# FFN input blocks of a two-layer decoder trunk: one 512-column matmul for the rounded weights instead of two of 256

## What is computed

```
for l in (0, 1):
    h = h + 0.5 * swiglu(rms_norm(h, ffn1_norm), ffn1_w_in, ffn1_w_out)
    u = rms_norm(h, mix_norm)
    ...  four mixers on projections of u, gated, summed over branches
    h = h + mixed @ w_out
    h = h + 0.5 * swiglu(rms_norm(h, ffn2_norm), ffn2_w_in, ffn2_w_out)

swiglu(u): a, b = split(u @ w_in);  (silu(a) * b) @ w_out        # width 2816 inside
```

## Time and profile before

| | us |
|---|---|
| median of 3 runs | 1290.23 (1284.02 to 1292.07) |
| the profiled execution, as timed | 1289.22 |
| its span in the trace | 1287.3 |
| PE busy | 1245.8 (97%) |
| DVE busy | 895.5 (70%) |
| ACT busy | 640.0 (50%) |
| PE's waits on w_lo_t, the longest kind | 15.0, of them 14.1 at the start |

### The profile page before, as it was taken

How to read it: one execution, slowest core, us unless ns; L and a number is a source line. 1 busy time by engine, 2 the same in 40 slices (tenths; PEclk the granted TensorE clock), 3 DMA queues, 4 the chain that set the end, 5 groups by cost and what they waited for, 6 DMA issues and landing times.

```text
span 1287.3 us, 25597 instructions
## 1 busy us (share of the span) xinstructions
PE 1245.8 (97%) x10328; PEld 1222.4 (95%) x10328; DVE 895.5 (70%) x1172; ACT 640.0 (50%) x904; POOL 327.4 (25%) x462
## 2 busy tenths in 40 slices
PE   5999999999999999999999999999999999999998
PEld 5999999888999999999999999998889999999998
DVE  4766857877877676555676687687887786656554
ACT  5654545663544454444456445557625444534432
POOL 0388800364003300000005895005630041000000
PEclk9999999998999999999999999999999999999999
DMA  7555554542344365555545545544333454555541
GB/s 299 199 185 174 180 179 165 175 149 99 131 158 166 135 236 198 191 195 168 191 135 201 188 165 200 189 164 152 135 130 131 154 186 160 201 184 175 186 173 66
DMA packets 31029, 220.46 MB, mean 171 GB/s; under 512 B 3568, under 2 KB 3568, under 8 KB 4592
## 3 DMA queue, kind: packets, MB, share of 16 engines
q1 hardware_dynamic: 30960, 219.49, 49.0%
HBM read 218.42 MB, written 1.05 MB: 170 GB/s over the span
## 4 chain that ended last, share of the span: by engine, by line
PE 75%; DVE 12%; POOL 7%; ACT 3%; issue 2%; DMA 0%; DVEq 0%; SPq 0%; ACTq 0%
PE banks L456 24%; PE banks L457 24%; PE banks L458 24%; DVE w_lo_t L1072 5%; PE banks L469 3%; ACT w_hi_t L812 1%; POOL st L1631 1%; DVE s5x L1274 1%; POOL s5x L1629 1%; POOL s5x L1628 1%; POOL st L1634 1%; POOL st L1536 1%; POOL st L1632 1%; DVE u_lo_t L1084 1%; DVE hT L1223 1%
## 5 line engine op out<-in xcount | busy, mean ns | idle before, releaser
L1072 DVE TENSOR_TENSOR w_lo_t<-raw,w_hi_t 128x1024 fp32r<-128x1024 f32 x408 | 518.0, 1310 | 107.8 <-ACT w_hi_t L812 107.4
L812 ACT ACTIVATE w_hi_t<-raw 128x1024 fp32r<-128x1024 f32 x408 | 407.2, 1046 | 126.7 <-PE banks L458 126.0
L456 PE MATMUL banks<-u_hi_t,w_hi_t 128*128 128x256 f32 x1520 | 436.0, 287 | 18.2 <-DVE w_lo_t L1072 14.1
L457 PE MATMUL banks<-u_lo_t,w_hi_t 128*128 128x256 f32 x1520 | 431.9, 284 | 0.0
L458 PE MATMUL banks<-u_hi_t,w_lo_t 128*128 128x256 f32 x1520 | 431.9, 284 | 0.0
L456 PEld LDWEIGHTS banks<-u_hi_t,w_hi_t 128*128 128x128 f32 x1520 | 293.6, 193 | 22.5 <-DVE w_lo_t L1072 14.1
L457 PEld LDWEIGHTS banks<-u_lo_t,w_hi_t 128*128 128x128 f32 x1520 | 293.8, 193 | 0.1
L458 PEld LDWEIGHTS banks<-u_hi_t,w_lo_t 128*128 128x128 f32 x1520 | 293.5, 193 | 0.0
L456 PE MATMUL banks<-b_hi_t,w_hi_t 128*128 128x256 f32 x864 | 245.1, 284 | 1.9 <-DVE b_lo_t L1084 1.9
L457 PE MATMUL banks<-b_lo_t,w_hi_t 128*128 128x256 f32 x864 | 244.5, 283 | 0.0
L458 PE MATMUL banks<-b_hi_t,w_lo_t 128*128 128x256 f32 x864 | 244.5, 283 | 0.0
(11 more groups left out here) (215 smaller groups left out, 1267.7 us busy)
## 6 DMA issues: line engine op xcount, KB each, us to landing
raw<-weights SPq DMA_DIRECT2D x203, 1024.0 KB, 4.9
prm<-params SPq DMA_DIRECT2D x1, 1178.5 KB, 5.3
prm<-params SPq DMA_DIRECT2D x1, 1166.5 KB, 15.1
cst<-constants SPq DMA_DIRECT2D x1, 1027.0 KB, 11.1
hT<-x_t SPq DMA_DIRECT2D x2, 512.0 KB, 5.5
raw<-weights SPq DMA_DIRECT2D x2, 512.0 KB, 6.4
out_t<-hT SPq DMA_DIRECT2D x4, 256.0 KB, 2.2
prm<-params SPq DMA_DIRECT2D x1, 12.0 KB, 1.9
```

Source lines behind the costliest of these rows:

```text
L456: pe.matmul(o, st[0], mv[0], start=start, stop=False, skip_group_check=True)
L457: pe.matmul(o, st[0], mv[1], start=False, stop=False, skip_group_check=True)
L812: act.activation(w_hi[:, slot, a:a + HALF], raw[:, slot, a:a + HALF], ACT.Copy) \
L1072: dve.tensor_tensor(w_lo[:, slot, a:a + HALF], raw[:, slot, a:a + HALF], w_hi[:, slot, a:a + HALF].bitcast(F32), ALU.subtract).then_inc(s. ...
```

## The change

The two parts of u stand side by side in one tensor now (`u_t`, and `b_t` for f = 1), so that one matmul with 512 columns passes the rounded weights over both: its result fills a whole bank, columns 0 to 255 with hi by hi, columns 256 to 511 with hi by lo. A second matmul of 256 columns adds the rest of the weights by the hi part to the first half. An input block of an FFN thus takes two banks, one for a and one for b. Before `scale`, ACT copies the second halves of both banks into `ab` (`correction`), DVE adds the first halves to that, and DVE then multiplies with `rstd_row` in a second instruction. The blocks of the mixers and the output blocks stay as they were. The banks are 4 and 5 for j = 0, 0 and 1 for j = 1, 2 and 3 for j = 2, then 6 and 7 for odd and 4 and 5 for even j. PE waits before output block 0 until DVE has added the halves of j = 2 (`h_raw`).

```diff
...
@@ -238,11 +240,9 @@
         w_lo = sb("w_lo_t", [P, RING, BLK], F32R)
         hT = sb("hT", [P, KT, T])
         U = sb("U", [P, KT, T])
-        u_hi = sb("u_hi_t", [P, KT, T], F32R)
-        u_lo = sb("u_lo_t", [P, KT, T], F32R)
+        u_t = sb("u_t", [P, 2, KT, T], F32R)
         G = sb("G", [P, 4, KT, T])
-        b_hi = sb("b_hi_t", [P, 4, 2, T], F32R)
-        b_lo = sb("b_lo_t", [P, 4, 2, T], F32R)
+        b_t = sb("b_t", [P, 2, KT, T], F32R)
         h_hi = sb("h_hi_t", [P, 2, T], F32R)
         h_lo = sb("h_lo_t", [P, 2, T], F32R)
         cst = sb("cst", [P, NCONST])
@@ -274,9 +274,11 @@
         ab, hf = sbqk, yb[:, :, 0, :]
-        tiles8 = lambda x: x.rearrange("p n k t -> p (n k) t")
-        in_hi = [u_hi[:, :, :], tiles8(b_hi[:, :, :, :])]
-        in_lo = [u_lo[:, :, :], tiles8(b_lo[:, :, :, :])]
+        u_hi, u_lo = u_t[:, 0, :, :], u_t[:, 1, :, :]
+        b_hi, b_lo = (b_t[:, i, :, :].rearrange("p (n k) t -> p n k t", n=4) for i in range(2))
+        in_t = [u_t, b_t]
+        in_hi = [x[:, 0, :, :] for x in in_t]
+        in_lo = [x[:, 1, :, :] for x in in_t]
         end_hi = [x[:, 6:8, :] for x in (in_hi[1], in_hi[0])]
         end_lo = [x[:, 6:8, :] for x in (in_lo[1], in_lo[0])]
         mix_hi = [(h_hi if dt < 2 else u_hi)[:, dt, :] for dt in range(KT)]
...
@@ -485,13 +489,34 @@
                     block_ready(b)
                     in_part(b, slot, bank, where, range(KT), tiles)
+                def wide_part(slot, bank, where, kts):
+
+
+                    for kt in kts:
+                        for ct in range(2):
+                            st = w(slot, kt * 256 + ct * P, P)
+                            last = kt == KT - 1 and ct == 1
+                            pe.matmul(banks[:, bank + ct, :], st[0], in_t[where][:, :, kt, :],
+                                      start=kt == 0, stop=False, skip_group_check=True)
+                            ins = pe.matmul(banks[:, bank + ct, 0:T], st[1], in_hi[where][:, kt, :],
+                                            start=False, stop=kt == KT - 1, skip_group_check=True)
+                    if last:
+                        ins.then_inc(s.w_used, 1)
+
+                def wide_block(b, slot, bank, where):
+                    block_ready(b)
+                    wide_part(slot, bank, where, range(KT))
+
                 def first_two(b, bank, norm, where):
                     for n, (j, q) in enumerate(STRAIGHT):
                         if q == 0:
                             block_ready(b + j)
                         pe.wait_ge(s.u_lo, layer * PER.u_lo + 4 * norm + q + 1)
-                        in_part(b + j, (b + j) % 3, bank + j, where, (2 * q, 2 * q + 1))
+                        if norm == 1:
+                            in_part(b + j, (b + j) % 3, bank[j], where, (2 * q, 2 * q + 1))
+                        else:
+                            wide_part((b + j) % 3, bank[j], where, (2 * q, 2 * q + 1))
                         if n == SS_AFTER:
                             sum_squares(norm)
                         if n == ROW_AFTER:
@@ -541,28 +566,30 @@
                                   first and dt % 2 == 0, False, s.w_used if last else
                                   (s.ffn_acc if tiles_first and k == 1 and dt % 2 == 1 else None))
-                    first_two(b0, 4, 2 * f, f)
+                    first_two(b0, (4, 0), 2 * f, f)
                     def body(i, first):
                         if first:
-                            in_block(b0 + 2, (b0 + 2) % 3, 6, where=f)
+                            wide_block(b0 + 2, (b0 + 2) % 3, 2, f)
                         else:
                             pe.wait_ge(s.h_ab, layer * PER.h_ab + FT * f + 2 * i - 1)
-                            in_block(b0 + 3 * i - 1, (b0 + 2) % 3, 4, where=f)
+                            wide_block(b0 + 3 * i - 1, (b0 + 2) % 3, 4, f)
+                        if first:
+                            pe.wait_ge(s.h_raw, layer * PER.h_raw + FT * f + 3)
                         out_block(0 if first else i - 1, b0 + 3 * i, b0 % 3, False)
                         pe.wait_ge(s.h_ab, layer * PER.h_ab + FT * f + 2 * i)
-                        in_block(b0 + 3 * i + 1, (b0 + 1) % 3, 5, where=f)
+                        wide_block(b0 + 3 * i + 1, (b0 + 1) % 3, 6, f)
                     body(1, True)
                     with pe.Fori(2, FT // 2 - 1) as i:
                         body(i, False)
                     pe.wait_ge(s.h_ab, layer * PER.h_ab + FT * f + FT - 3)
-                    in_block(b0 + FFN_BLOCKS - 4, (b0 + 2) % 3, 4, where=f)
+                    wide_block(b0 + FFN_BLOCKS - 4, (b0 + 2) % 3, 4, f)
                     pe.wait_ge(s.h_ab, layer * PER.h_ab + FT * f + FT - 2)
-                    in_block(b0 + FFN_BLOCKS - 3, b0 % 3, 5, where=f)
+                    wide_block(b0 + FFN_BLOCKS - 3, b0 % 3, 6, f)
                     out_block(FT // 2 - 2, b0 + FFN_BLOCKS - 2, (b0 + 1) % 3, False)
                     out_block(FT // 2 - 1, b0 + FFN_BLOCKS - 1, (b0 + 2) % 3, True, end_hi[f], end_lo[f])
@@ -747,7 +774,7 @@
                             branch_block(b, int(SEQ[m][3]))
                             continue
                         if m == 0:
-                            first_two(b, 0, 1, 0)
+                            first_two(b, (0, 1), 1, 0)
                             continue
                         if m >= 2:
                             prev = EVACUATED[EVACUATED.index(m) - 2]
@@ -844,6 +871,14 @@
             for layer in range(LAYERS):
                 own = Steps(act, s.act, layer, PER.act)
+                def correction(f, j, buf, k, slot, bank=None):
+
+                    act.wait_ge(s.w_used, layer * PER.w_used + RING * k + slot + 1 + RING)
+                    if not (isinstance(j, int) and j < 2):
+                        act.wait_ge(s.h_prod, layer * PER.h_prod + FT * f + j - 1)
+                    bank = 4 + 2 * buf if bank is None else bank
+                    act.activation(ab[:, buf, :, :], banks[:, bank:bank + 2, T:2 * T], ACT.Copy).then_inc(s.h_corr, 1)
+
                 def silu(f, j, buf):
                     act.wait_ge(s.h_ab, layer * PER.h_ab + FT * f + j + 1)
                     act.activation(ab[:, buf, 0, :], ab[:, buf, 0, :], ACT.Silu).then_inc(s.h_silu, 1)
@@ -857,9 +892,11 @@
                 def ffn(f):
                     k0 = ffn_steps(f)
+                    correction(f, 0, 0, k0, 0, 4)
                     silu(f, 0, 0)
                     hidden_hi(f, 0, 0)
                     round_weights(layer, k0 + 1, 0)
+                    correction(f, 1, 1, k0, 1, 0)
                     silu(f, 1, 1)
                     hidden_hi(f, 1, 1)
                     round_weights(layer, k0 + 1, 1)
@@ -867,16 +904,18 @@
                         act.wait_ge(s_params, (layer + 1) * 16)
                         act.activation(s5n[:, 0, :], p_("log_step"), ACT.Exp).then_inc(s.s5_exp, 1)
-                    def body(i):
+                    def body(i, bank=None):
+                        correction(f, 2 * i, 0, k0 + i - 1, 2, bank)
                         silu(f, 2 * i, 0)
                         round_weights(layer, k0 + i, 2)
                         hidden_hi(f, 2 * i, 0, k0 + i, 0)
                         round_weights(layer, k0 + i + 1, 0)
+                        correction(f, 2 * i + 1, 1, k0 + i, 1)
                         silu(f, 2 * i + 1, 1)
                         hidden_hi(f, 2 * i + 1, 1)
                         round_weights(layer, k0 + i + 1, 1)
-                    body(1)
+                    body(1, 2)
                     if f == 0:
                         act.wait_ge(s.s5_red, layer * PER.s5_red + 1)
@@ -888,9 +927,11 @@
                     with act.Fori(2, FT // 2 - 1) as i:
                         body(i)
                     i = FT // 2 - 1
+                    correction(f, FT - 2, 0, k0 + i - 1, 2)
                     silu(f, FT - 2, 0)
                     round_weights(layer, k0 + i, 2)
                     hidden_hi(f, FT - 2, 0, hi=end_hi[f])
+                    correction(f, FT - 1, 1, k0 + i, 0)
                     silu(f, FT - 1, 1)
                     hidden_hi(f, FT - 1, 1, hi=end_hi[f])
                     if (layer, f) == (LAYERS - 1, 1):
@@ -1163,8 +1204,12 @@
                     dve.wait_ge(s.w_used, layer * PER.w_used + RING * (k) + slot + 1 + RING)
                     if not (isinstance(j, int) and j < 2):
                         dve.wait_ge(s.h_prod, layer * PER.h_prod + FT * f + j - 1)
-                    bank = 4 + buf if bank is None else bank
-                    dve.tensor_tensor(ab[:, buf, :, :], banks[:, bank, :].rearrange("p (c t) -> p c t", c=2),
+                    bank = 4 + 2 * buf if bank is None else bank
+                    both = banks[:, bank:bank + 2, :].rearrange("p c (n t) -> p c n t", n=2)
+                    dve.wait_ge(s.h_corr, layer * PER.h_corr + FT * f + j + 1)
```

(13 more changed lines are left out.)

## The result

The changed kernel takes 1314.27 us (median of 4 runs, 1311.27 to 1317.08) against 1289.94 for the kernel before, measured alongside: 1.0196 times as long, 95% interval 1.0151 to 1.0241. It is slower, by 1.5 to 2.4%; I had forecast no change, and 1306 as the end of the range.

A forecast was written before the change was run, and what follows sets the result against it. PE's matmul stream, with the weight load as what binds, was taken to bound the kernel. 1289.2 - 29.2 (stream) + 23.7 (stops) + 6.0 (clock) = 1289.7 profiled, 1290.7 as median; range 1275 to 1306.

The forecast's parts named there:

- part 1: PE's stream in the FFNs' input blocks: a wide-narrow pair takes 0.336 us in place of 0.360, saving 29.2 us.
- each matmul carries a fixed 0.013: Bound on the pair in PE's stream: 0.347 us, a gain of 13 ns, 15.8 us in all.
- the term of 24 ns: Gain per wide-narrow pair in PE's stream, over 1216 pairs: 29.2 us.
- part 2: New stop of PE before output block 0, waiting for DVE's addition of j = 2: 23.7 us over four FFNs.
- part 3: PE's clock falls to half after each of the four stops: 4 x 1.5 = 6.0 us lost (0 to 7).
- part 4: ACT's copies and DVE's additions cost nothing; in the loops the chain to `h_lo` grows 1.3 us but stays covered.
- (d): Before each output block 0, Silu's table reloads after each copy, up to 2 x 1.28 us more: 1301; chance 0.10.
- (a): In PE's stream the weight load alone binds, at 0.112 us: 38.9 us gained, 1281.0; chance 0.22 with or without clock drop.
- (b): PE's clock stays up after the stops: 1284.7, with (a) 1275.0; chance 0.09 alone.
- (c): Wide matmul in PE's stream takes 0.240 us, no gain: 1319.9; with a fixed 0.013 it is 1304; chance 0.13, both sizes.

The follow-up runs named there:

- experiment 1: Trunk left out, x copied to the output, only TensorE running 48 matmuls of each of nine shapes: fp32r 512 columns 227 ns, alternating 512/256 pair 353 ns.
- Experiment 4: Changed kernel with input block 2 of each FFN in banks 4 and 5, output block 0 waiting only for the addition of j = 1: 1291.39 us, 1.0000 times before.
- Experiment 7: Kernel with input block 2 in banks 4 and 5, four multiplications left out of GpSimd's last two doublings of the rotation tables: 1288.74 us, one execution.

## Why the prediction was wrong

**The bound of PE's stream, part 1: right to call for a price, wrong in the price.** I took the weight load for what binds, so that a wide matmul would hide its successor's and cost 0.216 us. The rival that I gave 13 ns a pair, "each matmul carries a fixed 0.013", is nearly what the bare stream shows: an fp32r matmul of 256 or more columns costs its columns plus 13.4 ns, the wide one too. By that alone the pair is 347. The last 6 ns come from alternating the widths. The step that failed is the term of 24 ns; 6.7 was measured, 8.1 us in place of 29.2. The profiled execution took 1311.7 us where I had worked out 1289.7, 22.0 less, and these 21.1 us are nearly all of that. The rest nearly cancels: 1.4 less for the stops, 1.1 more for the clock, 5.9 more in the loops and, by luck, 4.5 less in the mixers. What misled me was the unsplit float32 rows: they have 3 ns on top, as bf16 has in experiment 1, but the fixed cost belongs to fp32r. That loads came every 0.112 us there and fp32r matmuls every 0.120 was the sign that something besides the load costs time, and I gave it to the load. The half-clock row shows no fixed cost, but it says nothing of one at full clock.

By the Trainium skill, "TensorE: Matmul & The Clock Gate", section "Back-to-back issue gap", an isolated matmul has a gap of N/2.4 + 2.5 ns, with no word on the type. The bf16 rows of experiment 1 agree (109 and 216), the fp32r rows are 11 ns above it. Its 131 ns for a sustained stream at 512 columns was not seen in any run.

**The stop, part 2: right.** 23.7 us worked out, 22.3 measured; the second, third and fourth within 0.2 us, the first 1.1 too long. Experiment 4 takes it away with other banks alone and gets back 23 us, the clock's share included.

**The clock, part 3: right, a little small.** 6.0 us worked out, 7.1 measured. Half clock lasted up to 6.8 us where I had 3.4, but a part of it fell into the idle time.

**No cost in the loops, part 4: wrong for f = 0.** 5.9 us were lost there. I had counted on some 1.5 us of cover with VectorE's usual durations and left POOL out. Two things met: the chain to `h_lo` is longer, and its new multiplication reads two SBUF operands. In the kernel before, `scale` read a bank; no row of it was over 0.693 us, while the new multiplication had 11 of 88 above 0.72 and the longest at 2.17. The product and `hidden_lo` had long rows beside POOL before, too, up to 0.98 and 1.55 us, so the change added a third operation that can wait for POOL to a chain that already had two. Experiment 7, with fewer of POOL's large operations, has no loop wait; its one execution, and the ends of the long rows, fixed behind POOL's, show that POOL's large tiles are the cause. The Trainium skill, "VectorE: DVE Perf Modes", section "Two Vector instructions with no wait between them", has a second SBUF read interface, shared with GpSimd, for the second of two SBUF inputs; the rows agree with that: the PSUM reader beside POOL kept its length, while the rows with two SBUF inputs ended 0.28 or 0.55 us after POOL's.

**Rivals.** (d), Silu's table: there are 16 more table loads than before, now ahead of the copies in the loops, but I found no wait of PE behind one. (a) and (b) didn't happen. (c) came in, between its two sizes: 1304 at a pair of 347 ns, 1312 at 353, 1318 with the loop waits, and 1313 with the mixers' clock of the profiled execution. Measured were 1311.7 in that one (1312 on the same scale, 1.0 less) and 1314.3 in the median.

## What to carry to other kernels

In this stream, merging two fp32r matmuls saves only the fixed cost of one: 13.4 ns in 360, less 6 for mixing widths, and the extra bank traffic, additions and waits have to be paid from it. Where a merge doubles the banks that a block takes, look first at which accumulator it now has to queue behind: here the stop, not the work, was the loss. And when an operation's source moves from PSUM to SBUF, look whether its cover still holds when it has to wait for a running GpSimd operation.

## What the runs showed that I had not expected

- An fp32r matmul carries 13.4 ns beyond its columns at full clock (256: 120, 384: 173.5, 512: 227 ns), a bf16 one 2.5 (109 and 216), and at half clock fp32r shows none (213). It depends neither on layout, nor on work of VectorE, ScalarE and the DMA engines, nor on whether each load brings another tile. In experiment 1 the rows of the weight loads differ with the type too, 188 to 192 ns for fp32r and 98 for bf16. What the 13.4 ns are stays open.
- Mixed widths cost on top: 512 with 256 alternately 353 (347 due), two and two 348, four and four 351, 512 with 384 413 (400 due), 384 with 256 293 (294 due). No rule of mine fits all five; it stays open.
- Fp32r 512 and bf16 256 in turns take 357 ns, more than two fp32r ones.
- VectorE's 128x512 multiplication with both inputs in SBUF took up to 2.17 us beside GpSimd's 128x1024 operations, the addition with one input in PSUM never more than 0.69. A row of 256 columns with both inputs in SBUF that starts while a large GpSimd operation runs (with more than 0.15 us of it left) ends 0.28 us after it, one of 512 columns 0.55 us, in the kernel before as in the changed one.
